# The borders between layers: order of k tiles, banks, sums and weight copies in a two-layer trunk

## The reference

```python
def rms_norm(x, gain):
    y = xf * lax.rsqrt(jnp.mean(xf * xf, axis=-1, keepdims=True) + NORM_EPS)
    return y * gain

def stick_breaking_attention(q, k, v, scale):      # per block of 128 queries
    z = jnp.einsum('bqhd,bkhd->bhqk', q, k) * scale
    sp = jnp.where(mask, jax.nn.softplus(z), 0.0)
    tail = lax.cumsum(sp, axis=3, reverse=True) - sp
    w = jnp.where(mask, jnp.exp(jax.nn.log_sigmoid(z) - tail), 0.0)
    return jnp.einsum('bhqk,bkhd->bqhd', w, v)

def stick_breaking_mixer(h, w_in, w_out):
    q, k, v = jnp.split(h @ w_in, 3, axis=-1)
    return stick_breaking_attention(q, k, v, C_HEAD_DIM ** -0.5) @ w_out

def swiglu(h, w_gate, w_up, w_down):
    return (jax.nn.silu(h @ w_gate) * (h @ w_up)) @ w_down

for l in range(2):
    x = x + mixer[l](rms_norm(x, norm_mix[l]))
    x = x + swiglu(rms_norm(x, norm_ffn[l]), w_gate[l], w_up[l], w_down[l])
```

## Time and profile before

| | |
|---|---|
| median of 3 runs | 1336.61 us (1335.61 to 1336.84) |
| the profiled execution | 1336.34 us |
| its span | 1334.5 us |
| PE busy | 1281.6 us |
| DVE, ACT, POOL busy | 598.0, 574.6, 514.0 us |
| transfers | 105.84 MB, mean 79 GB/s |
| first network starts | 290.2 us |
| layer 1's first projection starts | 660.1 us |
| its output projection ends, second network starts | 964.9 us |

### The profile page before, as it was taken

One profiled execution on the slowest core, in us unless ns is written; L12 is line 12 of the kernel. 1 busy time (PEld: TensorE's weight loads), 2 busy tenths in 40 slices (PEclk: granted clock), 3 DMA queues, 4 the chain that ended last, 5 costly groups with the idle time before them and its releaser, 6 DMA issues.

```text
span 1334.5 us, 16920 instructions
## 1 busy us (share of the span) xinstructions
PE 1281.6 (96%) x6308; PEld 1076.2 (81%) x6308; DVE 598.0 (45%) x1033; ACT 574.6 (43%) x953; POOL 514.0 (39%) x223
## 2 busy tenths in 40 slices
PE   8888898999999999999989999998999999999999
PEld 8788887778888888888868888886888888888887
DVE  7877777753221112222168888887222220122210
ACT  5656665643332122233366777776333331222310
POOL 5432411164445434445522222221644453344441
PEclk9889998999999999999989999999999999999999
DMA  5220111022223222233111111110323332233331
GB/s 207 72 64 33 33 47 33 16 91 95 95 101 115 84 79 94 94 118 103 65 62 48 47 63 47 49 61 17 104 88 98 98 122 89 71 98 100 102 129 40
DMA packets 29143, 105.84 MB, mean 79 GB/s; under 512 B 3360, under 2 KB 3616, under 8 KB 29088
## 3 DMA queue, kind: packets, MB, share of 16 engines
q1 hardware_dynamic: 28944, 105.07, 23.9%
q10 hardware_dynamic: 144, 0.02, 0.0%
HBM read 102.98 MB, written 2.10 MB: 79 GB/s over the span
## 4 chain that ended last, share of the span: by engine, by line
PE 66%; DVE 17%; ACT 10%; issue 5%; POOL 1%; DMA 0%; ACTq 0%; DVEq 0%; SPq 0%; POOLq 0%
PE bank L342 19%; PE bank L343 19%; PE bank L346 19%; DVE cs_hi L1477 2%; DVE cs_lo L1479 2%; ACT ca L1435 1%; ACT ca L1433 1%; ACT w_hi L318 1%; ACT cq_hi L1516 1%; DVE pt_lo L1080 1%; POOL ssum L436 1%; ACT pn L1066 1%; ACT pn L1054 1%; DVE cs L1445 1%; DVE tiny L1185 1%
## 5 line engine op out<-in xcount | busy, mean ns | idle before, releaser
L330 POOL TENSOR_TENSOR w_lo<-wraw,w_hi 128x1024 fp32r<-128x1024 f32 (+4 forms) x180 | 458.6, 2549 | 751.8 <-ACT w_hi L318 751.8
L342 PE MATMUL bank<-h_hi,w_hi 128*128 128x512 f32 x896 | 353.8, 395 | 1.0 <-DVE h_lo L426 1.0
L343 PE MATMUL bank<-h_lo,w_hi 128*128 128x512 f32 x896 | 351.6, 392 | 0.0
L318 ACT ACTIVATE w_hi<-wraw 128x1024 fp32r<-128x1024 f32 (+4 forms) x180 | 197.3, 1096 | 158.2 <-DVE x L633 128.7
L346 PE MATMUL bank<-h_hi,w_lo 128*128 128x512 f32 x896 | 223.4, 391 | 0.0
L342 PEld LDWEIGHTS bank<-h_hi,w_hi 128*128 128x128 f32 x896 | 168.9, 188 | 38.6 <-DVE h_lo L426 1.6
L346 PEld LDWEIGHTS bank<-h_hi,w_lo 128*128 128x128 f32 x896 | 168.3, 188 | 37.0
L343 PEld LDWEIGHTS bank<-h_lo,w_hi 128*128 128x128 f32 x896 | 168.9, 189 | 36.0
L342 PE MATMUL bank<-f_hi,w_hi 128*128 128x512 f32 x352 | 138.3, 393 | 0.0
L343 PE MATMUL bank<-f_lo,w_hi 128*128 128x512 f32 x352 | 138.3, 393 | 0.0
L619 DVE TENSOR_TENSOR fu<-bank,rstd 128x512 f32<-128x512 f32 x44 | 30.4, 691 | 200.3 <-PE bank L346 200.3
(11 more groups left out here) (272 smaller groups left out, 2015.9 us busy)
## 6 DMA issues: line engine op xcount, KB each, us to landing
wraw<-in_w_in SPq DMA_DIRECT2D x120, 512.0 KB, 3.3
wraw<-in_w_down SPq DMA_DIRECT2D x32, 704.0 KB, 4.1
wraw<-in_w_ab SPq DMA_DIRECT2D x20, 512.0 KB, 3.3
x<-in_xt SPq DMA_DIRECT2D x8, 256.0 KB, 6.9
out<-x SPq DMA_DIRECT2D x8, 256.0 KB, 2.0
wraw<-in_w_ab SPq DMA_DIRECT2D x4, 416.0 KB, 6.8
wraw<-in_w_ab SPq DMA_DIRECT2D x2, 384.0 KB, 3.1
wraw<-in_w_ab SPq DMA_DIRECT2D x2, 256.0 KB, 2.9
```

The costliest lines, as they stand in the source:

```text
L318: nc.scalar.activation(whi[:, s, 0:width], wraw[:, s, 0:width], ACT.Copy).then_inc(S("w_hi"), 1)
L330: nc.gpsimd.tensor_tensor(wlo[:, s, 0:width], wraw[:, s, 0:width], whi[:, s, 0:width], ALU.subtract).then_inc(S("w_lo"), 1)
L342: nc.tensor.matmul(out_bank, w, src_hi[kt], start=(kt == 0), stop=False)
L343: nc.tensor.matmul(out_bank, w, src_lo[kt], start=False, stop=False)
```

## The change

1. In a first chunk (`first` given) the last k tile is taken out: high and low products of the other tiles run, then those of the last tile.
2. In the first network sums and spread come one chunk later (`SUM_AFTER`); in the second they stay.
3. The squares have 4 buffers instead of 2.
4. In the networks ACT's copy of the chunk three ahead stands before the Silu.
5. In the first pair v is projected into bank 3, k is copied and split before ACT's three weight copies, and `cyv` is waited for before the scores of head 1.
6. In each pair head 1's first weights (ACT: the first two blocks) go before the split of k, and ACT's third block before the weight copy.
7. The output projection has six banks. Chunk 2's first 7 k tiles run early too, tile by tile, behind the last pair's values.

```diff
@@ placement
-    sqn, end = place("sqn", [P, 2, SEQ], F32, at=vb0 + 512)
+    sqn, end = place("sqn", [P, 4, SEQ], F32, at=vb0 + 512)
@@ project
-        for kt in range(n):
-            if first is not None:
-                first(kt)
+
+        def high(kt):
             w = whi[:, s, kt * P:(kt + 1) * P]
             nc.tensor.matmul(out_bank, w, src_hi[kt], start=(kt == 0), stop=False)
             nc.tensor.matmul(out_bank, w, src_lo[kt], start=False, stop=False)
+
+        def low(kt):
+            return nc.tensor.matmul(out_bank, wlo[:, s, kt * P:(kt + 1) * P], src_hi[kt], start=False,
+                                    stop=(kt == n - 1))
+        early = n if first is None else n - 1
+        for kt in range(early):
+            if first is not None:
+                first(kt)
+            high(kt)
         pe.wait_ge(S("w_lo"), g + 1)
-        for kt in range(n):
-            last = nc.tensor.matmul(out_bank, wlo[:, s, kt * P:(kt + 1) * P], src_hi[kt],
-                                    start=False, stop=(kt == n - 1))
+        for kt in range(early):
+            last = low(kt)
+        if first is not None:
+            first(n - 1)
+            high(n - 1)
+            last = low(n - 1)
@@ norm_act
-        if d >= 2:
-            act.wait_ge(*at_norm(n, "sum", max(1, d - 2)))
-        nc.scalar.activation(sqn[:, d % 2, :], x[:, d, :], ACT.Square).then_inc(S("norm_sq"), 1)
+        if d >= 4:
+            act.wait_ge(*at_norm(n, "sum", max(1, d - 4)))
+        nc.scalar.activation(sqn[:, d % 4, :], x[:, d, :], ACT.Square).then_inc(S("norm_sq"), 1)
@@ output projection
-    OUT_BANK = (6, 2)
-    OUT_EARLY = 2
+    OUT_BANK = (6, 2, 0, 1, 6, 7, 6, 7)
+    OUT_EARLY = 3
...
-            if d >= 2:
-                pe.wait_ge(S("out_x"), L * KT + d - 1)
+            if d in (4, 6, 7):
+                pe.wait_ge(S("out_x"), L * KT + (1 if d == 4 else d - 1))
@@ ffn_pe
-                        if f == 0:
-                            if c == 0:
-                                norm_pe(pe, n, 7)
-                            else:
-                                rs_spread_pe(pe, f"n{n}", 7)
+                        if 2 * f + c == SUM_AFTER[L]:
+                            norm_pe(pe, n, 7)
+                        elif 2 * f + c == SUM_AFTER[L] + 1:
+                            rs_spread_pe(pe, f"n{n}", 7)
@@ ffn_act
+                split_ahead(3)
                 act.wait_ge(*at_net(L, "y", f + (s * HALF_F + 1)))
                 nc.scalar.activation(fs[:], fy[:], ACT.Silu).then_inc(S("net_s"), 1)
-
-                split_ahead(3)
@@ c_proj_bank
-        return bank[(CP, *ZB[0])[c]] if is_first(u) else bank[CP]
+        return bank[(CP, ZB[0][0], ZB[1][0])[c]] if is_first(u) else bank[CP]
@@ c_act
                     c_slot_act(act, nxt, "q")
+                    if u is None:
+                        c_slot_act(act, nxt, "k")
                     hi(0)
@@ c_pe
                     c_scores_pe(pe, u, 0)
+                    if is_first(u):
+                        pe.wait_ge(S("c_vy"), 1)
                     c_scores_pe(pe, u, 1)
...
                     out_early_pe(pe, G_OUT1, 1, 0, (KT - 2,))
+                    out_early_pe(pe, G_OUT1, 1, 2, range(KT - 1))
 
             c_pe(None, 0)
-            pe.wait_ge(S("c_vy"), 1)
```

More of the change, by code:

```diff
@@ L435, in norm_pool @@
             pool.wait_ge(*at_norm(n, "sum", d - 1))
-        nc.gpsimd.tensor_tensor(ssum[:], sqn[:, 0, :] if d == 1 else ssum[:], sqn[:, d % 2, :],
+        nc.gpsimd.tensor_tensor(ssum[:], sqn[:, 0, :] if d == 1 else ssum[:], sqn[:, d % 4, :],
                                 ALU.add).then_inc(S("norm_sum"), 1)
@@ L445, in norm_sum_dve @@
             dve.wait_ge(*at_norm(n, "sum", d - 1))
-        nc.vector.tensor_tensor(ssum[:], sqn[:, 0, :] if d == 1 else ssum[:], sqn[:, d % 2, :],
+        nc.vector.tensor_tensor(ssum[:], sqn[:, 0, :] if d == 1 else ssum[:], sqn[:, d % 4, :],
                                 ALU.add).then_inc(S("norm_sum"), 1)
@@ L467, in need_h, with out_bank @@
         return first
-    OUT_BANK = (6, 2)
-    OUT_EARLY = 2
+    OUT_BANK = (6, 2, 0, 1, 6, 7, 6, 7)
+    OUT_EARLY = 3
+    def out_bank(d):
+        return bank[OUT_BANK[d]][:]
     def out_early_pe(pe, g0, L, d, tiles):
-        project_tiles(pe, g0 + d, bank[OUT_BANK[d % 2]][:], m_hi, m_lo, tiles)
+        project_tiles(pe, g0 + d, out_bank(d), m_hi, m_lo, tiles)
     def out_pe(pe, g0, L, heads_done):
@@ L480, in out_pe @@
         for d in range(KT):
-            b = bank[OUT_BANK[d % 2]][:]
+            b = out_bank(d)
             if d < OUT_EARLY:
@@ L497, in out_dve @@
             dve.wait_ge(S("chunk_done"), g0 + d + 1)
-            nc.vector.tensor_tensor(x[:, d, :], bank[OUT_BANK[d % 2]][:], x[:, d, :],
+            nc.vector.tensor_tensor(x[:, d, :], out_bank(d), x[:, d, :],
                                     ALU.add).then_inc(S("out_x"), 1)
@@ L505, in trunk @@
     GU_LOOP = HALF_F // 3 * 3
+    SUM_AFTER = (1, 0)
     def ffn_each(eng, body):
@@ L1814, in c_act @@
                         c_w_act(act, u, 0, b)
-                if nxt is not None:
+                    for b in range(2):
+                        c_w_act(act, u, 1, b)
+                if nxt is not None and u is not None:
                     c_slot_act(act, nxt, "k")
@@ L1818, in c_act @@
                     c_lower_act(u, 0)
+                    c_w_act(act, u, 1, 2)
                 if nxt is not None:
@@ L1821, in c_act @@
                 if u is not None:
-                    for b in range(3):
-                        c_w_act(act, u, 1, b)
                     cout_act(u, 0)
@@ L2019, in c_dve @@
                 if nxt is not None:
+                    if u is None:
+                        c_y_dve(dve, nxt, "k")
                     c_slot_dve(dve, nxt, "q")
@@ L2025, in c_dve @@
                         c_w_dve(dve, u, 0, b)
+                if nxt is not None and u is not None:
+                    c_y_dve(dve, nxt, "k")
+                if u is not None:
+                    c_w_dve(dve, u, 1, 0)
                 if nxt is not None:
-                    c_y_dve(dve, nxt, "k")
                     c_slot_dve(dve, nxt, "k")
@@ L2030, in c_dve @@
                     c_out(u, 0)
-                    for b in range(3):
+                    for b in range(1, 3):
                         c_w_dve(dve, u, 1, b)
```

## The result

| | before | changed |
|---|---|---|
| median | 1336.11 us (1334.36 to 1336.84, 4 runs) | 1315.93 us (1313.19 to 1317.06, 4 runs) |
| the profiled execution | 1336.34 | 1317.06 |
| its span | 1334.5 | 1315.3 |
| PE busy | 1281.6 | 1272.7 |

The ratio of the changed kernel to the one before is 0.9848, with a 95% interval of 0.9828 to 0.9868: 20.2 us less, 1.5%. In a second measurement it was 1315.41 and 0.9852 (0.9839 to 0.9866).

A forecast was written before the change was run, and what follows sets the result against it. TensorE, busy 96% of the span, was taken to bound the kernel with its instruction stream plus holes. Gains of 5.6 + 3.9 + 7.5 + 2.4 = 19.4 us from 1336.6 gave 1317.2 us, forecast range 1314.5 to 1320.5 (0.60).

The follow-up runs named there:

- e4: Changed kernel with the first pair's second weight copy behind head 0's chain and the third behind head 1's; 1316.21 us, 0.9859 of the kernel before.
- e8: Changed kernel with two first-pair weight copies before the chain, the third and next pair's first behind the first weights' exponentials; 1312.38 us, 0.9824 of the kernel before.

## What to carry to other kernels

A wait that is removed on an engine off the critical path can let POOL run earlier, onto DVE's instructions. Look up for each POOL instruction with SBUF operands which DVE instruction it will now meet, and whether that one reads a bank or only SBUF. When copies are moved, place them by that and not just by "later": e4 moved the collisions and won nothing, e8 placed copies in gaps and won 3.5 us. And read the gain of a border by what the next engine allows behind it, as the gain in the first pair was cut twice, by a new hole and by the slow clock behind it.

## What was not expected of the hardware

- The fourteen profiles have 28 holes of PE of 2.1 us or more from the first network on, and 24 of them were followed by some microseconds at 1.2 instead of 2.4 GHz (a granted clock of 0.50 to 0.69 in the 4.5 us that follow). The four exceptions are three times the last pair's hole of 3.2 us and one of 2.17. The eight of 1.70 and the shorter ones (0.8 to 1.0) were never followed by one.
- Beside POOL's `w_lo` (2.4 us) an instruction of DVE with two inputs from SBUF took up to 2.9 us instead of 0.7. One that read a bank took no longer (0.55).
